# A mixer and expert kernel on one core: the experts' down weights loaded as column halves, in two transfers a block

## What is computed

```python
def hierarchical_moe(h, w_rg, b_rg, w_re, b_re, w_gate, w_up, w_down):
    ...
    y = jnp.zeros(h.shape, jnp.float32)
    for gi in range(N_GROUPS):
        hid = jax.nn.silu(jnp.einsum('nd,edf->nef', h, w_gate[gi])) * jnp.einsum('nd,edf->nef', h, w_up[gi])
        y = y + jnp.einsum('nef,efd->nd', hid * comb[:, gi, :, None], w_down[gi])
    return y
```

## Time and profile before

| | |
|---|---|
| time, median of 3 runs | 1886.43 us (1886.24 to 1890.31) |
| the profiled execution | 1891.13 us |
| its span in the trace | 1889.1 us |
| PE / DVE / ACT / POOL busy | 89% / 48% / 33% / 7% |
| chain that ended last, by engine | PE 66%, DMA 18%, DVE 9%, ACT 6%, issue 2% |
| chain, the two weights of the experts that stand in it | w_exp_down 9%, w_exp_up 8% |

### The profile page before, as it was taken

How to read it: one execution, slowest core, us unless ns; L and a number is a source line. 1 busy time by engine, 2 the same in 40 slices (tenths; PEclk the granted TensorE clock), 3 DMA queues, 4 the chain that set the end, 5 groups by cost and what they waited for, 6 DMA issues and landing times.

```text
span 1889.1 us, 33313 instructions
## 1 busy us (share of the span) xinstructions
PE 1672.6 (89%) x14777; PEld 1340.5 (71%) x14777; DVE 906.2 (48%) x1227; ACT 626.2 (33%) x792; POOL 125.4 (7%) x103
## 2 busy tenths in 40 slices
PE   8999999999999999999989999799989766655665
PEld 6999998998899999899878886588854222212221
DVE  4445565664443566565674967987523111101111
ACT  4444544543434453555363131433303000100000
POOL 0500000000060000000003620000000000000000
PEclk9999999999999999999989999899999999888998
DMA  8552366744676335686433320100099999999998
GB/s 301 208 193 93 134 227 236 278 185 161 238 253 229 112 132 198 232 293 222 173 110 113 85 72 1 24 3 4 25 348 401 408 410 409 410 409 410 410 410 335
DMA packets 162258, 420.01 MB, mean 222 GB/s; under 512 B 14178, under 2 KB 35357, under 8 KB 159058
## 3 DMA queue, kind: packets, MB, share of 16 engines
q1 hardware_dynamic: 161698, 417.87, 59.7%
q10 hardware_dynamic: 432, 0.22, 0.0%
HBM read 416.18 MB, written 1.89 MB: 221 GB/s over the span
## 4 chain that ended last, share of the span: by engine, by line
PE 66%; DMA 18%; DVE 9%; ACT 6%; issue 2%; DVEq 0%; ACTq 0%
PE bank L1285 31%; DMA R<-w_exp_down 9%; DMA R<-w_exp_up 8%; PE bank L1453 3%; PE ps_s L1399 3%; PE ps_t L1399 3%; PE bank L1845 2%; PE ps_s L1453 2%; ACT w_high L1891 2%; PE bank L1471 2%; PE bank L1827 2%; PE ps_t L1453 2%; DVE w_low L2346 1%; PE ps_t L1471 1%; PE ps_s L1471 1%
## 5 line engine op out<-in xcount | busy, mean ns | idle before, releaser
L2346 DVE TENSOR_TENSOR w_low<-wring,w_high 128x2048 fp32r<-128x2048 f32 (+1 forms) x127 | 285.0, 2244 | 306.5 <-ACT w_high L1891 306.1
L1891 ACT ACTIVATE w_high<-wring 128x2048 fp32r<-128x2048 f32 (+1 forms) x127 | 236.2, 1860 | 334.9 <-PE bank L1285 302.6
L1285 PE MATMUL bank<-x_high,w_high 128*128 128x256 f32 x1600 | 324.5, 284 | 7.7 <-DVEq L2397 7.7
L1285 PE MATMUL bank<-x_low,w_high 128*128 128x256 f32 x1600 | 320.9, 282 | 0.0
L1285 PE MATMUL bank<-x_high,w_low 128*128 128x256 f32 x1600 | 319.0, 281 | 0.0
L1285 PEld LDWEIGHTS bank<-x_high,w_high 128*128 128x128 f32 x1600 | 246.3, 190 | 14.6 <-DVEq L2397 8.7
L1285 PEld LDWEIGHTS bank<-x_high,w_low 128*128 128x128 f32 x1600 | 247.2, 190 | 0.0
L1285 PEld LDWEIGHTS bank<-x_low,w_high 128*128 128x128 f32 x1600 | 246.0, 189 | 0.0
L1845 PE MATMUL bank<-R 128*32 128x512 f32 x640 | 91.3, 702 | 68.5 <-DMA R<-w_exp_up 49.7
L1845 PEld LDWEIGHTS bank<-R 128*32 128x32 f32 x640 | 19.3, 117 | 129.4 <-DMA R<-w_exp_up 71.3
L3081 DVE TENSOR_TENSOR R<-bank,R 128x512 f32<-128x512 f32 x8 | 5.5, 694 | 219.0 <-PE bank L1845 219.0
(11 more groups left out here) (693 smaller groups left out, 2928.4 us busy)
## 6 DMA issues: line engine op xcount, KB each, us to landing
wring<-w_in SPq DMA_DIRECT2D x29, 2048.0 KB, 8.3
R<-w_exp_up SPq DMA_DIRECT2D x24, 2048.0 KB, 24.0
R<-w_exp_down SPq DMA_DIRECT2D x24, 2048.0 KB, 23.8
wring<-w_up SPq DMA_DIRECT2D x22, 2048.0 KB, 9.1
R<-w_exp_gate SPq DMA_DIRECT2D x16, 2048.0 KB, 23.4
wring<-w_exp_gate SPq DMA_DIRECT2D x16, 2048.0 KB, 23.8
wring<-w_ada SPq DMA_DIRECT2D x12, 2048.0 KB, 10.3
wring<-w_down SPq DMA_DIRECT2D x10, 2048.0 KB, 7.8
```

The lines of the kernel that those rows point to most:

```text
L1285: mm = pe.matmul(b[:, i * S:(i + 1) * S], left, right, start=k == 0 and m == 0 and i == 0, stop=k == last and m == 2, skip_group_check=True)
L1891: a.activation(high_of(l, job), half_block(l, job, wring), ACT.Copy).then_inc(w_high_ready, 1)
L2346: v.tensor_tensor(half_block(l, job, w_low), half_block(l, job, wring), high_of(l, job).bitcast(F32), ALU.subtract).then_inc(w_low_ready, 1)
```

## The change

Block c of the four down blocks now holds one half of the columns (half c // 2) and two quarters of the rows (the first two for even c, the last two for odd c). PE's matmuls are as many and as large as before; a block's eight now all go into one bank, and the first bank is complete after the second block. DVE scales it then, and PE distributes the first half behind the third block, the second half behind the fourth. A block is loaded by two transfers of 1 MB, one for each quarter of the rows, and its pieces are 512 numbers, 2 KB. Where both run, the two transfers raise the semaphore of the place twice; `expert_loads` counts that.

```diff
@@ expert_loads
-            each = 16 * 2 * TURN_BLOCKS // SLOTS_X
+            assert SLOTS_X == TURN_BLOCKS
             i = expert_slot(m)
-            earlier_loads = NB1 // SLOTS + (6, 6, 3, 3)[i] if i < SLOTS else 0
-            return sw_ * (TURNS // 2 * each) + pair * each + 16 * (earlier_loads + m // SLOTS_X + 1)
+            each = 16 * (2 if m % TURN_BLOCKS >= 2 * QUAD else 1)
+            earlier_loads = 16 * (NB1 // SLOTS + (6, 6, 3, 3)[i]) if i < SLOTS else 0
+            return sw_ * (TURNS * each) + pair * (2 * each) + (earlier_loads + each * (m // SLOTS_X + 1))
@@ load_pair (SP)
-                        k = (2, 2, 1)[which]
...
-                        sp.dma_start(expert_block(m).rearrange("p (u k n) -> p u k n", u=QUAD, k=k),
-                                     src[:, :, k * c:k * c + k, :]).then_inc(loaded[s], 16)
+                        block_of = expert_block(m).rearrange("p (u k n) -> p u k n", u=QUAD, k=2)
+                        if which < 2:
+                            sp.dma_start(block_of, src[:, :, 2 * c:2 * c + 2, :]).then_inc(loaded[s], 16)
+                        else:
+                            for k in range(2):
+                                sp.dma_start(block_of[:, :, k, :], src[:, :, c % 2 * 2 + k, c // 2 * 512:c // 2 * 512 + 512])\
+                                    .then_inc(loaded[s], 16)
@@ expert_turn (PE)
-                for k in range(D_EXP // P):
-                    m = m0 + 2 * QUAD + k
+                for c in range(QUAD):
+                    half, m = c // 2, m0 + 2 * QUAD + c
                     pe.wait_ge(loaded[expert_slot(m)], expert_loads(sw_, pair, m))
-                    ww = expert_block(m).rearrange("p (u n) -> p u n", u=QUAD)
-                    for half in range(2):
+                    ww = expert_block(m).rearrange("p (u k n) -> p u k n", u=QUAD, k=2)
+                    for k in (c % 2 * 2, c % 2 * 2 + 1):
                         for u in range(QUAD):
...
                     mm.then_inc(moe_used, 1)
-                for j in range(4):
-                    half, t = j // 2, j % 2
-                    if t == 0:
+                    if c >= 2:
+                        half = c - 2
                         pe.wait_ge(yg_dve, turn(sw_, pair, odd, half + 1, 2))
-                    pe.matmul(banks8[BACK[j]], putT[:, t, :], yg[:, half * 512:(half + 1) * 512], start=True, stop=True)\
-                        .then_inc(moe_full, 1)
+                        for t in range(ST):
+                            pe.matmul(banks8[BACK[2 * half + t]], putT[:, t, :], yg[:, half * 512:(half + 1) * 512], start=True,
+                                      stop=True).then_inc(moe_full, 1)
@@ expert_turn (DVE)
-                v.wait_ge(moe_used, used_by(sw_, pair, m0 + TURN_BLOCKS))
                 for half in range(2):
                     c = slice(half * 512, (half + 1) * 512)
+                    v.wait_ge(moe_used, used_by(sw_, pair, m0 + 2 * QUAD + 2 * (half + 1)))
                     v.tensor_tensor(yg[:, c], banks8[5 + half], gmoe[:, c], ALU.mult).then_inc(yg_dve, 1)
-                for j in range(4):
-                    half, t = j // 2, j % 2
-                    hv = h[:, t, half * 512:half * 512 + 512]
-                    v.wait_ge(moe_full, turn(sw_, pair, odd, 5 + j, 8))
-                    v.tensor_tensor(hv, hv, banks8[BACK[j]], ALU.add).then_inc(y_done, 1)
+                    for t in range(ST):
+                        j = 2 * half + t
+                        hv = h[:, t, c]
+                        v.wait_ge(moe_full, turn(sw_, pair, odd, 5 + j, 8))
+                        v.tensor_tensor(hv, hv, banks8[BACK[j]], ALU.add).then_inc(y_done, 1)
```

More of the change, by code:

```diff
@@ L1852, in expert_turn @@
                 pe.wait_ge(hidT_ready, turn(sw_, pair, odd, 1, 1))
-                for k in range(D_EXP // P):
-                    m = m0 + 2 * QUAD + k
+                for c in range(QUAD):
+                    half, m = c // 2, m0 + 2 * QUAD + c
                     pe.wait_ge(loaded[expert_slot(m)], expert_loads(sw_, pair, m))
-                    ww = expert_block(m).rearrange("p (u n) -> p u n", u=QUAD)
-                    for half in range(2):
+                    ww = expert_block(m).rearrange("p (u k n) -> p u k n", u=QUAD, k=2)
+                    for k in (c % 2 * 2, c % 2 * 2 + 1):
                         for u in range(QUAD):
                             q = slice(SLOTS_E * u, SLOTS_E * (u + 1))
-                            mm = pe.matmul(banks8[5 + half][q, :], hidT[:, k, q], ww[:, u, half * 512:(half + 1) * 512],
-                                           start=k == 0, stop=k == D_EXP // P - 1)
+                            mm = pe.matmul(banks8[5 + half][q, :], hidT[:, k, q], ww[:, u, k % 2, :], start=k == 0,
+                                           stop=k == D_EXP // P - 1)
                     mm.then_inc(moe_used, 1)
-                for j in range(4):
-                    half, t = j // 2, j % 2
-                    if t == 0:
+                    if c >= 2:
+                        half = c - 2
                         pe.wait_ge(yg_dve, turn(sw_, pair, odd, half + 1, 2))
-                    pe.matmul(banks8[BACK[j]], putT[:, t, :], yg[:, half * 512:(half + 1) * 512], start=True, stop=True)\
-                        .then_inc(moe_full, 1)
+                        for t in range(ST):
+                            pe.matmul(banks8[BACK[2 * half + t]], putT[:, t, :], yg[:, half * 512:(half + 1) * 512], start=True,
+                                      stop=True).then_inc(moe_full, 1)
             keep_clock(banks8[3], ident[:, :], h[:, 1, 512:1024], 2)
```

## The result

| | before | after |
|---|---|---|
| median | 1887.91 us (7 runs, 1885.74 to 1890.62) | 1895.1 us (7 runs, 1892.11 to 1896.4) |
| ratio | | 1.0032, 95% interval 1.0018 to 1.0045 |
| the profiled execution, its span | 1891.13, 1889.1 us | 1896.4, 1894.4 us |

The ratio is 6.0 us on the time before (3.4 to 8.5), and the medians alone differ by 7.2; 6.2 was forecast. As a time 1892.6 us was forecast, on a time before of 1886.43; 1895.1 lies inside the range given, 1888.2 to 1896.2. A second measurement of the same kernel, beside the experiments, gave 1897.08 us (6 runs), just above that range, and a ratio of 1.0047 (1.0031 to 1.0064), or 8.9 us. So the cost is there, and between 3 and 12 us.

The account below looks back on a forecast made before the run. The prediction took the full DMA stream of expert weights as the bound: +7.9 us for the stream and -1.7 for the tail gave +6.2, so 1886.43 became 1892.6 us, range 1888.2 to 1896.2.

Parts of the forecast that it names:

- The bound: Expert part, from about 1400 us on: full DMA engines streaming the weights set its length, at 410 GB/s.
- The stream, +7.9: Down loads of the expert part: 2 KB pieces in 32 of 96 blocks run slower, +7.9 us, ends +0 and +10.1.
- first block of each run at 400 GB/s: Each turn's four down blocks: the first at 400 GB/s (+0.125 us), the other three at 388 (+0.287 each).
- The 410 at 84 us: A single 2 KB load with nothing behind it ran at 410 GB/s; evidence against the dearer stream.
- The tail, -1.7: Behind the last block: only the second half's scaling and two of four distributing matmuls remain, so the store comes 1.7 us sooner.
- clock rival: Kernel's end: last block or first half's distribution meets PE's low clock, up to 1.3 us more, 1893.9 us; chance 0.12.
- Transfers at nothing: SP's queue and the DMA engines: 32 more transfers and their completion writes are priced at nothing.
- Stream free: Each turn's down loads run at 408 to 410 GB/s, costing 0 to 0.7 us; 1884.7 to 1885.4 us; chance 0.13.
- all like the first of a run: Every down block runs at 400 GB/s, +4.0 us, less 1.7: +2.3, 1888.7 us; chance 0.10.
- The rule on 512 B: Transfers from 512 B reach line rate, so 2 KB pieces would cost nothing and the sum would be -1.7 us.
- Dearer than any row: Down loads cost twice the extra taken, more than any 2 KB load in the trace: +14.1 us, 1900.5; chance 0.05.
- What would show it: Expert part's trace: about 402 GB/s, 124.8 us over two turns, 7.9 us behind the last landing, stretches before 1400 us unmoved.

Follow-up runs that it names:

- e4: Kernel before, with all 96 weight blocks loaded in two transfers of 2 KB pieces; 1914.39 us, ratio 1.0140.
- e6: Kernel before, with each down block loaded in four transfers of 0.5 MB with 1 KB pieces; 1919.84 us, ratio 1.0168.
- e2: Kernel before, with each down block in two transfers cut between the experts, pieces still 4 KB; 1887.34 us, ratio 0.9999.
- e1: Kernel before, with only its down loads split into two column halves of 2 KB pieces, PE and DVE order unchanged; 1896.92 us, ratio 1.0053.
- e5: Kernel before, with every third block (gate, up and down alike) in two transfers of 2 KB pieces; 1897.94 us, ratio 1.0053.
- e9: Kernel before, with the last block's first half scaled earlier and blocks of two experts in 8 KB pieces; 1880.08 us, ratio 0.9955.
- e10: Kernel before, with earlier first-half scaling, gate and up blocks of one expert in 16 KB pieces, down blocks in 8 KB; 1877.91 us, ratio 0.9946.

## Why the prediction was right, point by point

- **The bound.** The expert part is set by the stream of weights. e4 and e6 change the loads alone, and the time follows: 26.4 us for 27.0 in the stream, 31.7 for 29.1 and 1.7 of tail.
- **The stream, +7.9.** The mechanism is right: the price is on the piece, not on the transfer (e2) and not on the order (e1). The size was low. The step that failed is the first block of each run at 400 GB/s, taken from w_out's first 4 us; these follow a pause of the engines, and e5 shows no such grace in a full queue. The 410 at 84 us that stood against the dearer stream was read over two microseconds of that load; behind them it runs at 393. At 387 GB/s for all 32 the term is 9.7, and e1's stream measured 9.8, inside the ends given (0 to 10.1). The changed kernel's own stream measured 10.6 and 11.0, a little above them; the last engine's lag and, in the first trace, PE's first half of the columns are in that.
- **The tail, -1.7.** 9.6 became 7.9 in both traces. The first half's work fitted ahead of the last block with the small margin that the sum had (1879.6 against 1879.8), and in one trace without any: the third block took 3.64 us where 3.20 was counted, PE was through at 1886.6, and the chain leads through it. The forecast's clock rival names this case, a first half that still holds PE; it cost some tenths of a us here and not 1.3.
- **Transfers at nothing.** Confirmed by e2: ratio 0.9999.
- **The sum.** With the right term it would have been 9.7 - 1.7 = +8.0 instead of +6.2. The two measurements gave 6.0 and 8.9, with intervals that hold both sums; so that the first came out at the forecast's number is partly luck. The time itself, 1895.1 against 1892.6, lies 2.5 us off, 1.5 of it because the kernel before measured 1887.91 this time and not 1886.43.
- **The rivals.** Stream free and all like the first of a run are ruled out (402 GB/s in e5, and no trace with 2 KB pieces above 404). The rule on 512 B of the Trainium skill (DMA: Bandwidth & Descriptors, section Specifications) doesn't hold for this stream: a fourfold length of that already loses 5.6%. Of the same page's cost for each packet, direction and kind are right and the size is not: 2.3% by my estimate against 5.6%. The clock rival did not come true for the last block here, but did in e5, e6 and e9, with 1.4 us and more. Dearer than any row: no.
- **What would show it.** 402 GB/s (found: 399 to 404), 124.8 us over two turns (125.3 and 126.3), 7.9 us of tail (7.9). That nothing moves before 1400 us was wrong as a test: that part scatters by over 4 us from one execution to the next.

What stays open: in both traces of the changed kernel the last block was taken 0.8 and 1.2 us later than in e1, whose loads have the same sizes. That is about the scatter between equal streams. The lag of the last engine (the rows under the table) and, in the first trace, PE's own first half have a part in it; the rest is not explained.

## To carry to other kernels

When a stage is held by a full transfer queue, price a change of layout by the length of the pieces that lie together in memory before its gain elsewhere: here halving them on a third of the data cost 9.8 us, for a tail of 1.7. Look for part of the tail gain without touching the layout (an earlier signal gave 0.8 us by the trace, at no cost that was seen), and try longer pieces first: 8 and 16 KB gave 0.45% and 0.54% on the whole kernel, the early signal included. Before half of a block is sent ahead, look in the trace whether half of its matmuls takes half of the time; cut between experts it took all of it. Compare traces from an event at the entrance of the stage, not by their spans.

## What the runs showed of the hardware

Beyond what was expected, the cost of a piece is nearly a constant from 1 KB to 8 KB. A block of 2.097 MB takes 5.12 us in 512 pieces. At 387 GB/s it takes 5.42 in 1024, at 348 it takes 6.03 in 2048, and at 421 it takes 4.98 in 256. Divided by the pieces' difference from 512 and multiplied by 16 engines, the cost for each piece is 9.4, 9.5 and 8.8 ns on its engine. Extrapolated to no pieces at all this leaves about 435 GB/s; e10's 427 with 16 and 8 KB mixed is on that line. The first microseconds of 2 KB loads behind a pause of the engines (410 GB/s at 84 us, 412 in e4 at 83 us, 400 in w_out's first 4) are off it, and this remains unexplained.
